# Two attentions of one kernel: scores asked for in pairs of heads, and the sink as a column beside the scores

## The reference

```python
def sliding_window_sink_attention(q, k, v, sinks):      # 8 heads of 64, 2 key heads, blocks of 128
    s = jnp.einsum('bnqkgd,bnjkd->bnkgqj', qb, kk) * (HEAD_DIM ** -0.5)
    s = jnp.where(valid[None, :, None, None], s, NEG)
    m = jnp.maximum(jnp.max(s, axis=-1, keepdims=True), sink)
    e = jnp.exp(s - m)
    p = e / (jnp.sum(e, axis=-1, keepdims=True) + jnp.exp(sink - m))
    o = jnp.einsum('bnkgqj,bnjkd->bnqkgd', p, vv)

def neighbourhood_attention(q, k, v, rpb):               # 8 heads of 64, rows of 64 columns
    s = jnp.einsum('bchd,bicjhd->bhcij', q_row, k_nb)
    s = s + bias[None]
    p = jax.nn.softmax(s.reshape(B, NA_HEADS, GRID_W, kh * NA_KW), axis=-1)
    return jnp.einsum('bhcij,bicjhd->bchd', p, v_nb)
```

## Time and profile before

| | us |
|---|---|
| median of three runs (3101.75 to 3108.52) | 3102.76 |
| the profiled execution | 3107.42 |
| its span | 3105.6 |
| TensorE busy in it (share 86%) | 2662.6 |
| VectorE busy (46%) | 1434.0 |
| ScalarE busy (27%) | 840.7 |
| the first attention, from and to | 195.6 to 277.7 |
| the second attention, from and to | 1832.9 to 2006.6 |

### The profile page before, as it was taken

How to read it: one execution, slowest core, us unless ns; L and a number is a source line. 1 busy time by engine, 2 the same in 40 slices (tenths; PEclk the granted TensorE clock), 3 DMA queues, 4 the chain that set the end, 5 groups by cost and what they waited for, 6 DMA issues and landing times. The chain is left out here.

```text
span 3105.6 us, 33740 instructions
## 1 busy us (share of the span) xinstructions
PE 2662.6 (86%) x12721; PEld 1854.6 (60%) x12721; DVE 1434.0 (46%) x2381; ACT 840.7 (27%) x1407; POOL 667.1 (21%) x421
## 2 busy tenths in 40 slices
PE   5987587999999997999999599865988788788886
PEld 2853466999999996888888466552322223223222
DVE  4345443998878775888888524433000000000001
ACT  2224121334666662333333222321000000000001
POOL 0030000667888882222222010000000000000000
PEclk8977788999999998999999799977999999999999
DMA  5433131555899999999999231119999999999996
GB/s 221 123 124 126 68 109 57 169 174 194 286 360 384 372 340 350 354 357 351 353 353 323 95 93 45 48 59 402 421 421 421 421 421 421 421 421 421 421 421 283
DMA packets 246772, 870.01 MB, mean 280 GB/s; under 512 B 28415, under 2 KB 97663, under 8 KB 194040
## 3 DMA queue, kind: packets, MB, share of 16 engines
q1 hardware_dynamic: 190048, 703.71, 59.0%
q0 software_dynamic: 38016, 138.43, 11.7%
q10 hardware_dynamic: 18584, 26.23, 2.3%
HBM read 812.69 MB, written 55.60 MB: 280 GB/s over the span
## 5 line engine op out<-in xcount | busy, mean ns | idle before, releaser
L687 PE MATMUL val_banks<-val_v,val_coef_split 128*128 128x512 f32 x2304 | 525.1, 390 | 17.8 <-DVE val_coef_split L87 17.8
L687 PEld LDWEIGHTS val_banks<-val_v,val_coef_split 128*128 128x128 f32 x2304 | 434.4, 189 | 108.4 <-DVE val_v L87 18.0
L932 PE MATMUL moe_up_ps<-all_raw_first,all_h_rows 128*64 128x512 f32 x1696 | 422.5, 608 | 73.1 <-DMA all_raw_first<-in_w_up 53.7
L566 PE MATMUL dots_dot_ps<-one_acts,dots_u_split 128*128 128x384 f32 x2064 | 374.8, 338 | 17.9 <-POOL dots_u_split L87 17.7
L566 PEld LDWEIGHTS dots_dot_ps<-one_acts,dots_u_split 128*128 128x128 f32 x2064 | 359.3, 189 | 21.1 <-POOL dots_u_split L87 11.0
L932 PEld LDWEIGHTS moe_up_ps<-all_raw_first,all_h_rows 128*64 128x64 f32 x1696 | 138.4, 139 | 324.3 <-issue 323.2
L87 POOL TENSOR_TENSOR dots_u_split<-dots_u_raw,dots_u_split 128x1024 fp32r<-128x1024 f32 x86 | 226.8, 2639 | 366.3 <-ACT dots_u_split L82 365.3
L1051 DVE TENSOR_TENSOR all_x<-moe_y_ps,all_x 128x512 f32<-128x512 f32 x64 | 44.1, 691 | 558.7 <-PE moe_y_ps L898 558.6
L949 PE MATMUL moe_y_ps<-all_raw_first,moe_hid_t 128*64 128x512 f32 x848 | 203.7, 597 | 43.2 <-DMA all_raw_first<-in_w_down 24.7
L82 ACT CAST val_v<-pe_shared 128x2048 fp32r<-128x2048 f32 x64 | 122.4, 1912 | 354.6 <-PE val_banks L687 345.9
L1121 POOL DMA_INDIRECT val_v_rows<-in_peer_v,one_expert x128 | 124.1, 970 | 409.5 <-DVE val_banks L638 389.1
(11 more groups left out here) (358 smaller groups left out, 3437.1 us busy)
## 6 DMA issues: line engine op xcount, KB each, us to landing
all_raw_first<-in_w_gate SPq DMA_DIRECT2D x106, 1024.0 KB, 27.3
all_raw_first<-in_w_up SPq DMA_DIRECT2D x106, 1024.0 KB, 27.6
all_raw_first<-in_w_down SPq DMA_DIRECT2D x106, 1024.0 KB, 27.3
pe_shared<-in_peer_v SPq DMA_DIRECT2D x64, 1024.0 KB, 7.3
dots_u_raw<-in_u_tiles SPq DMA_DIRECT2D x86, 512.0 KB, 4.4
expert_dots<-dots_gelu ACTq DMA_DIRECT2D x128, 192.0 KB, 4.3
expert_weights<-pe_shared SPq DMA_DIRECT2D x48, 512.0 KB, 10.6
pe_shared<-expert_dots SPq DMA_DIRECT2D x64, 384.0 KB, 7.3
```

Of the source, the lines that this page charges most:

```text
L566: last = self.nc.tensor.matmul(self.banks[:, q % 2, 0:DENSE], self.split[q % 3][:, u_part, k], self.h_t[:, h_part, k, T - DENSE:T], start= ...
L687: last = nc.tensor.matmul(banks[:, 2 * (t + 1) + half, :], coef_split[:, b, c_part, a, t * P:(t + 1) * P], v[:, b, v_part, a, half * BANK: ...
L932: last = nc.tensor.matmul(up_ps[of(e), b, :], xs_t(i)[:, k, of(e)], w[e][:, b * BANK:(b + 1) * BANK], start=(k == 0), stop=(k == KD - 1))
```

## The change

What it does:

- `pe_step` asks for scores in even steps alone, for unit i and unit i + 1 together. It waits for the biased scores of unit i - 1 (`biased_ready` at i, where it was i - 1).
- The units of the second attention are reordered, so that units i and i + 1 are an even and an odd head with the same queries' block. Four bias tables are held instead of two, of 15 x 64 columns instead of 16 x 64; the first two are asked for ahead of the weight tiles, the next two behind the transform's tables, with no wait for a unit.
- In the first attention the score tile has one more column in front, and eight places instead of three, one for each head. The negated sink of the head is written to that column once, by the operation that negated the sinks before. The biased scores' operation takes its start value from there, and the exponential runs over the sink's column too, so that its sum has the sink in it. The exponential of the sink alone (L1480), the add (L1501) and two semaphores go.

```diff
--- before.py
+++ after.py
...
 
-    def __init__(self, nc, s, ident, units, q_of, k_of, v_of, bias_of, o_of, keys_max, sinks=None, minus_sinks=None,
-                 bias_wait=None):
+    def __init__(self, nc, s, ident, units, q_of, k_of, v_of, bias_of, o_of, keys_max, sinks=0, bias_wait=None):
         self.nc, self.ident, self.units, self.n = nc, ident, units, len(units)
         self.q_of, self.k_of, self.v_of, self.bias_of, self.o_of = q_of, k_of, v_of, bias_of, o_of
-        self.sinks, self.minus_sinks, self.bias_wait = sinks, minus_sinks, bias_wait
+        self.first, self.bias_wait = (1 if sinks else 0), bias_wait
         self.steps = self.n + 3
         n = self.n
-        self.biased = s.sb("biased", [P, 3, keys_max])
-        self.expd = s.sb("expd", [P, 3, keys_max])
+        self.places = sinks or 3
+        self.biased = s.sb("biased", [P, self.places, self.first + keys_max])
+        self.expd = s.sb("expd", [P, 3, self.first + keys_max])
...
-        self.sink_exp = s.sb("sink_exp", [P, n])
         self.total_inv = s.sb("total_inv", [P, n])
...
+    def scores(self, i, keys):
+
+        return self.biased[:, i % self.places, self.first:self.first + keys]
 
     def pe_step(self, pe, i):
         nc = self.nc
-        if i < self.n:
-            keys = self.k_of(*self.units[i])
+        if i < self.n and i % 2 == 0:
             if i >= 2:
-                pe.wait_ge(self.biased_ready, i - 1)
-            nc.tensor.matmul(self.score_ps[:, i % 2, 0:keys.shape[1]], self.q_of(*self.units[i]), keys,
-                             start=True, stop=True).then_inc(self.scored, 1)
+                pe.wait_ge(self.biased_ready, i)
+            for u in (i, i + 1):
+                keys = self.k_of(*self.units[u])
+                nc.tensor.matmul(self.score_ps[:, u % 2, 0:keys.shape[1]], self.q_of(*self.units[u]), keys,
+                                 start=True, stop=True).then_inc(self.scored, 1)
         if 2 <= i < self.n + 2:
             j = i - 2
             pe.wait_ge(self.exp_ready, j + 1)
@@ -1446,7 +1451,7 @@
                 pe.wait_ge(self.turn_taken, j - 1)
             for c in range(self.k_of(*self.units[j]).shape[1] // P):
                 last = nc.tensor.transpose(self.turn_ps[:, j % 2, c, :],
-                                           self.expd[:, j % 3, c * P:(c + 1) * P], self.ident[:])
+                                           self.expd[:, j % 3, self.first + c * P:self.first + (c + 1) * P], self.ident[:])
             last.then_inc(self.turned, 1)
         if i >= 3:
             j = i - 3
@@ -1473,12 +1478,9 @@
             act.wait_ge(self.biased_ready, i + 1)
             if i >= 3:
                 act.wait_ge(self.turned, i - 2)
-            nc.scalar.activation(self.expd[:, i % 3, 0:kw], self.biased[:, i % 3, 0:kw], ACT.Exp, scale=-1.0,
-                                 bias=self.minus_top[:, i:i + 1],
+            nc.scalar.activation(self.expd[:, i % 3, 0:self.first + kw], self.biased[:, i % self.places, 0:self.first + kw],
+                                 ACT.Exp, scale=-1.0, bias=self.minus_top[:, i:i + 1],
                                  accum_out=self.total[:, i:i + 1]).then_inc(self.exp_ready, 1)
-            if self.sinks is not None:
-                nc.scalar.activation(self.sink_exp[:, i:i + 1], self.sinks(*self.units[i]), ACT.Exp,
-                                     bias=self.minus_top[:, i:i + 1]).then_inc(self.sink_ready, 1)
 
     def dve_step(self, dve, i):
         nc = self.nc
@@ -1487,20 +1489,15 @@
             if self.bias_wait is not None:
                 self.bias_wait(dve, i)
             dve.wait_ge(self.scored, i + 1)
-            if i >= 3:
-                dve.wait_ge(self.exp_ready, i - 2)
+            if i >= self.places:
+                dve.wait_ge(self.exp_ready, i - self.places + 1)
             nc.vector.tensor_tensor_reduce(
-                out=self.biased[:, i % 3, 0:kw], in0=self.score_ps[:, i % 2, 0:kw], in1=self.bias_of(*self.units[i]),
-                scale=-1.0, scalar=-LOWEST if self.minus_sinks is None else self.minus_sinks(*self.units[i]),
+                out=self.scores(i, kw), in0=self.score_ps[:, i % 2, 0:kw], in1=self.bias_of(*self.units[i]),
+                scale=-1.0, scalar=self.biased[:, i % self.places, 0:1] if self.first else -LOWEST,
                 op0=ALU.add, op1=ALU.min, accum_out=self.minus_top[:, i:i + 1]).then_inc(self.biased_ready, 1)
         if i >= 3:
             j = i - 3
             dve.wait_ge(self.exp_ready, j + 1)
-            if self.sinks is not None:
-                dve.wait_ge(self.sink_ready, j + 1)
-                nc.vector.tensor_tensor(self.total[:, j:j + 1], self.total[:, j:j + 1], self.sink_exp[:, j:j + 1],
-                                        ALU.add).then_inc(self.total_ready, 1)
-                dve.wait_ge(self.total_ready, j + 1)
             nc.vector.reciprocal(self.total_inv[:, j:j + 1], self.total[:, j:j + 1]).then_inc(self.inv_ready, 1)
             dve.wait_ge(self.inv_ready, j + 1)
             dve.wait_ge(self.weighed, j + 1)
...
         mask = s.sb("mask", [P, 2 * P])
         sinks = s.sb("sinks", [P, NH])
-        minus_sinks = s.sb("minus_sinks", [P, NH])
 
...
@@ -1735,8 +1731,7 @@
             k_of=lambda n, h: feat[part(h), 4 + h // 4, max(n - 1, 0) * P:(n + 1) * P],
             v_of=lambda n, h: [values[:, c, 64 * (h // 4):64 * (h // 4) + 64] for c in range(max(n - 1, 0), n + 1)],
             bias_of=lambda n, h: mask[:, P:2 * P] if n == 0 else mask[:],
-            o_of=lambda n, h: attn[:, n, DH * h:DH * h + DH], keys_max=2 * P,
-            sinks=lambda n, h: sinks[:, h:h + 1], minus_sinks=lambda n, h: minus_sinks[:, h:h + 1])
+            o_of=lambda n, h: attn[:, n, DH * h:DH * h + DH], keys_max=2 * P, sinks=NH)
...
             def _(dve):
                 nc.vector.memset(b_rows[:], 0.0).then_inc(b_zeroed, 1)
                 dve.wait_ge(mask_loaded, 32)
-                nc.vector.tensor_scalar(minus_sinks[:], sinks[:], -1.0, None, ALU.mult).then_inc(minus_ready, 1)
+                nc.vector.tensor_scalar(att.biased[:, :, 0], sinks[:], -1.0, None, ALU.mult).then_inc(minus_ready, 1)
                 dve.wait_ge(minus_ready, 1)
                 for i in range(att.steps):
                     att.dve_step(dve, i)
@@ -1875,19 +1870,21 @@
         return slice(64 * (h % 2), 64 * (h % 2) + 64)
 
     with Scope(nc, "mix2") as s:
-        table = s.sb("table", [P, 2, 16 * 64])
-        table_loaded = [s.sem(f"table_loaded{i}") for i in range(2)]
+        TABLES = 4
+        table = s.sb("table", [P, TABLES, 15 * 64])
+        table_loaded = [s.sem(f"table_loaded{i}") for i in range(TABLES)]
 
         def table_wait(dve, i):
-            if i % NT == 0:
-                dve.wait_ge(table_loaded[i // NT % 2], 16 * (i // NT // 2 + 1))
+            if i % (2 * NT) < 2:
+                h = 2 * (i // (2 * NT)) + i % 2
+                dve.wait_ge(table_loaded[h % TABLES], 16 * (h // TABLES + 1))
 
         att = Attention(
-            nc, s, ident, [(t, h) for h in range(NH) for t in range(NT)],
+            nc, s, ident, [(t, h + i) for h in range(0, NH, 2) for t in range(NT) for i in range(2)],
             q_of=lambda t, h: qk[part_of(h), h // 2, t * P:(t + 1) * P],
             k_of=lambda t, h: qk[part_of(h), 4 + h // 2, :],
             v_of=lambda t, h: [values[:, c, DH * h:DH * h + DH] for c in range(NT)],
-            bias_of=lambda t, h: table[:, h % 2, (7 - 2 * t) * 64:(7 - 2 * t) * 64 + T],
+            bias_of=lambda t, h: table[:, h % TABLES, (7 - 2 * t) * 64:(7 - 2 * t) * 64 + T],
             o_of=lambda t, h: attn[:, t, DH * h:DH * h + DH], keys_max=T, bias_wait=table_wait)
 
...
@@ -1944,15 +1941,15 @@
                     sp.dma_start(tile_raw[:, j % 3], w[:, :, at:at + P]).then_inc(w_loaded[j % 3], 16)
 
                 def head(h):
-                    sp.dma_start(table[:, h % 2, :], A["bias_table"][h]).then_inc(table_loaded[h % 2], 16)
+                    sp.dma_start(table[:, h % TABLES, :], A["bias_table"][h][:, 0:15 * 64]).then_inc(table_loaded[h % TABLES], 16)
 
                 head(0)
+                head(1)
                 for j in range(3):
                     tile(j)
...
-                head(1)
                 for g, half in enumerate(group_rows):
...
@@ -1965,14 +1962,14 @@
                     if j == 5:
                         for i, name in enumerate(("dft_cos", "dft_sin")):
                             sp.dma_start(trig[:, i], A[name].rearrange("(t p) f -> p t f", p=P)).then_inc(trig_loaded, 16)
-                        sp.wait_ge(att.biased_ready, NT)
                         head(2)
+                        head(3)
                 sp.wait_ge(lo_ready, 8)
                 sp.dma_start(filt, spec_dram).then_inc(filt_loaded, 16)
-                for h in range(3, NH):
-                    sp.wait_ge(att.biased_ready, NT * (h - 1))
+                for h in range(TABLES, NH):
```

(20 more changed lines are left out.)

## The result

The changed kernel took 3069.03 us (median of 4 runs, 3067.25 to 3073.93), the kernel before 3105.27 beside it: ratio 0.9885, 95% interval 0.9869 to 0.9902. So 36.2 us were won, where 27.6 and a time of 3075.2 were forecast. The profiled execution took 3073.93 us, its span 3072.1.

The account below looks back on a forecast made before the run. TensorE was taken to bound the second attention and the first from 226 on, VectorE before that. First attention 16.7 plus second 10.9 gave 27.6 off 3102.76, so 3075.2 us; range 3063 to 3093.

Parts of the forecast that it names:

- Overlap: Both attentions: a pair's scores lie in different partition halves and run together, so the second score costs 0.
- staggered: Score pairs in both attentions: half an overlap, instructions staggered by one; 18.1 us won, 3084.7; chance 0.12.
- serial rival: Score pairs in both attentions: no overlap, a pair costs nearly twice 1.05; 8 us won, 3095; chance 0.08.
- First attention, the sink: 3.7 + 0.4: Sink add and its waits go, giving TensorE 3.7 us; the sink's separate exponential goes, 0.4 at the start.
- First attention, the clock: 3: Without the stalls TensorE is dense from 204 and its clock may rise earlier: between 0 and 7 us, taken as 3.
- Scores at the high clock, and the end: First attention: seven scores saved in steps 13 to 25, 4.4 us; steps 27, 29, 31 limited by the gate, 0.7.
- Second attention: Start, saved odd scores and the stalls of its middle steps, together 10.9 us won.
- the start: Second attention: head 1's table stands ahead of the first raw weight tile on SP's queue; a loss of 1.3 us.
- Steps 16 to 20: Second attention: pairs wait behind the spectrum, two stalls of some 2.5 us; loss 0 to 3, taken as 1.5.
- Pairs behind unit 22: Second attention, late steps: each odd score saved gives 1.1 us, and VectorE keeps up by 0.16.
- A stage outside moves: Sign of being wrong: a stage outside the two attentions moves, or the two together shrink by under 18 or over 37 us.
- the main case: Whole kernel: pairs overlap fully, 27.6 us won, median 3075.2, ends 3066 to 3083; chance 0.72.

Follow-up runs that it names:

- e5: Kernel after, but the second attention's pairs are two neighbours of one head, both in the same half of the partitions: 3083.68 us.
- e1: Kernel before with the sink column alone; scores one at a time, second attention as before: 3110.13 us.
- e12: e1 with GpSimd's convolution of the first attention left out, its result filled with zeros: 3107.09 us.
- e6: Kernel after, but the first attention's heads are reordered so that both scores of a pair lie in one half of the partitions: 3076.54 us.
- e9: Kernel after, but the first attention's odd score is issued behind the even step's transposes, so pairs are split: 3090.08 us.
- e3: Kernel before with the second attention's part of the change only; first attention as before: 3091.80 us.
- e4: Kernel before with pairs in the first attention only, the sink still exponentiated and added by two instructions: 3096.16 us.
- e7: e4 with GpSimd's convolution of the first attention left out, its result filled with zeros: 3082.68 us.
- e10: Kernel after with first weight tile before second table, sinks negated on ScalarE, spectrum in four pieces in odd steps, transform back in steps 22 and 24: 3063.75 us.
- e8: Kernel after with first weight tile before second table, sinks negated on ScalarE, spectrum in steps 14, 16 and 18: 3069.81 us.
- e11: Kernel after with two edits only: first weight tile before second table, sinks negated on ScalarE: 3071.54 us.

## Why the prediction was right, and where its sizes were off

- **Overlap.** Right, at 128, 256 and 512 columns; neither the staggered nor the serial rival came. The evidence of one row at 128 columns carried over to 512; that it would was a bet, as before had no wider pair of two halves. The row it was contrasted with was read wrongly: 2.79 us for two scores of one head was set beside 1.12 at 2.4 GHz, but the granted clock fell from 1.00 to 0.50 within that row (from 1834.0 on). At 2.4 GHz throughout such a pair takes 1.98 (e5), still nearly twice one score.
- **First attention, the sink: 3.7 + 0.4.** The waits went, and up to unit 12 e1 was 4.8 us ahead, but at the end of the stage nothing was left of it (90.2 against 88.4), as the clock rose later. I counted a stall as a price of its own; it is one only where what follows runs as fast without it.
- **First attention, the clock: 3.** This is the term that was mis-sized. Up to the ninth piece of weights the kernel after was 18.8 us ahead (49.1 and 30.3 after the first score) where my terms gave 12.9 with the clock's 3 in them; so, with the other terms as they were, the clock gave 8.9. I had set it between 0 and 7, with a rise at step 7 at best; it came in step 4. The reason I gave, that the stalls keep the clock low, was half of it: without them the clock still rose late while scores were single (e1, e12).
- **Scores at the high clock, and the end.** From the ninth to the sixteenth piece 3.1 us were won, five scores at 0.63 as reckoned; behind it 0.9 (0.7 forecast).
- **Second attention.** Up to unit 16, 6.0 us were won (110.9 and 104.9; 6.1 forecast): the start cost 1.7 and not 1.3, and 1.3 more at the low clock, and the seven pairs gave the rest, 9.0, or 1.3 each and not 1.05. The Trainium skill (TensorEngine Tiling (Array Packing), Key Properties) has a change of tiling mode drain the engine. By that rule I had 1.19 for a pair. The plain steps give exactly that (2 x 2.48 - 3.77), and e5's 0.34 for mere neighbours is more than the 0.14 that I set down for it. That it is a drain no run shows: e5 has neighbours of one half in place of separate ones, and nothing tells a drain from another cost of the change.
- **Steps 16 to 20.** The two waits came, 2.65 and 0.89, where two of 2.5 were forecast: TensorE ran at the low clock between them (score 2.08) and was itself late for the second. Between units 16 and 22 the kernel after took 23.5 (e6 and e9 too, e3 25.2), and the six without pairs 23.7 to 27.1, by how long their own clock stayed low. I forecast a loss of 0.4 with step 21's score; the profile of before against after gives a gain of 3.6, others anything down to a loss of 1.4. What this stretch gives is a matter of the clock in the single execution.
- **Pairs behind unit 22.** 26.8 to 22.0 for four pairs, 1.2 each (1.1 forecast). VectorE kept up.
- **A stage outside moves.** By two of my own tests I would be wrong. 4.6 us were missing between the attentions, and the two stages together shrank by 38.5 us, where more than 37 was to say that I am wrong. The first test was set too fine for one profile: the fourteen differ by that much there. The second was passed through the clock's 5.9 above its term, and because the profile of before had the longest second attention of six; with the 12.2 of the middles the two stages give 35.1.
- **The sum and the range.** 36.2 us were won and 27.6 forecast. Of the 8.6 between them 5.9 are the clock's term and 1.3 lie in the second attention (12.2 by the middles, 10.9 forecast). The upper end of the main case, 3083, is 3 us more than its terms give (3075.2 + 3 + 1.5).

What stays open is why the clock stays low under single scores, with no gap in TensorE's rows. With two scores side by side, overlapping or not, the rise comes at 208 to 216 us. With the two split (e9) it comes at 219, but the clock falls again at 260. The rows show modelled ends, and so can't show gaps of a tenth of a microsecond inside a step. Nor did I try to raise the clock in the single form by filling the array otherwise.

## What to carry to other kernels

Where operands of 64 partitions lie in both halves, issue such matmuls in pairs, right behind each other: here the second was free (1.13 us for four matmuls of 512 columns, 1.12 for two), and the clock rose some 30 us sooner. Reckon a stall not by its length but by the clock behind it: in e4 four waits, 8.3 us together, cost 14.3 (against e7). Work that is moved into a loop of pairs is better placed behind both consumers of a pair and in small pieces: the waits were 0.47, 0.34 and 0.34 so (e10), and 0.64, 1.95 and 1.49 between them (e8), in one profile each.

## What the runs showed of the hardware

- The clock stayed at 1.2 GHz over 45 us in which TensorE's rows have no gap (e1 from 205, e12 from 206), and with two overlapping scores in every other step it was at 2.4 GHz 14 us after the first score.
- A tensor add of one column took 3.90 us beside a GpSimd tensor operation and 0.16 without (e4, e7); reciprocals (0.16) and evictions from PSUM (0.28) took the same beside one as without.
- The same stall of 2.65 us had 3.4 us of low clock behind it in one execution (after) and 13.6 in another (e11), which cost 4.0 us more.
- Two f32 scores of 512 columns, each from 64 partitions, took 1.13 us from different halves and 1.98 from the same half (after, e5).
